# x loaded in 32-by-32 squares and turned on VectorE instead of TensorE, in a decoder block

## The reference

```python
h = rms_norm(x, norm_g) * (1.0 + scale) + shift        # scale, shift, gate from silu(c) @ w_ada + b_ada
proj = h @ w_in                                        # 1024 -> 3592 columns: u, z_pool, q, k, v, o, z_mlstm, gates
pool_out = causal_pool_mixer(u) * silu(z_pool)         # trailing means over 2/4/8/16 positions
qk = silu(causal_depthwise_conv(q, k))                 # width 4
hm = mlstm_chunkwise(q, k, v, gates)                   # 4 heads, chunks of 128 positions, one after the other
mlstm_out = head_norm(hm) * sigmoid(o) * silu(z_mlstm)
x = x + gate * (concat[pool_out, mlstm_out] @ w_out)
out = rms_norm(x, final_g)
```

## Time and profile before

| | |
|---|---|
| median of 3 runs | 1848.31 us (1847.39 to 1850.02) |
| profiled execution, its own time | 1848.88 us |
| span in the profile | 1847.1 us |
| TensorE busy | 1809.6 us (98%) |
| VectorE busy | 1013.3 us (55%) |
| ScalarE busy | 521.5 us (28%) |
| GpSimd busy | 262.1 us (14%) |
| granted TensorE clock, mean | 0.994 |
| bytes over the DMA queues | 336.85 MB, mean 182 GB/s |

### The profile page before, as it was taken

How to read it: one execution, slowest core, us unless ns; L and a number is a source line. 1 busy time by engine, 2 the same in 40 slices (tenths; PEclk the granted TensorE clock), 3 DMA queues, 4 the chain that set the end, 5 groups by cost and what they waited for, 6 DMA issues and landing times.

```text
span 1847.1 us, 25117 instructions
## 1 busy us (share of the span) xinstructions
PE 1809.6 (98%) x9537; PEld 1554.0 (84%) x9537; DVE 1013.3 (55%) x2247; ACT 521.5 (28%) x1054; POOL 262.1 (14%) x229
## 2 busy tenths in 40 slices
PE   6989999999999999999999999999999999999998
PEld 5878889888898888988888888888889888898886
DVE  6685684527736276353863357452673627735383
ACT  3344331332323132222222223132222313222221
POOL 3433222040210003000030001200022000300000
PEclk9899999999999999999999999999999999999999
DMA  9896735595256552665427653466535665266431
GB/s 329 272 313 181 239 116 181 165 327 194 93 189 194 191 186 85 211 203 178 155 91 242 203 193 104 163 204 216 179 99 189 187 198 189 78 212 202 150 124 69
DMA packets 144348, 336.85 MB, mean 182 GB/s; under 512 B 13068, under 2 KB 55012, under 8 KB 144228
## 3 DMA queue, kind: packets, MB, share of 16 engines
q1 hardware_dynamic: 129028, 312.56, 50.9%
q10 hardware_dynamic: 15200, 22.68, 4.1%
HBM read 288.86 MB, written 46.33 MB: 181 GB/s over the span
## 4 chain that ended last, share of the span: by engine, by line
PE 88%; DVE 7%; issue 2%; ACT 1%; DMA 1%; SPq 0%; POOL 0%; ACTq 0%; DVEq 0%; POOLq 0%
PE ps_acc L511 23%; PE ps_acc L513 23%; PE ps_acc L512 23%; PE ps_kv L511 2%; PE ps_kv L512 2%; PE ps_kv L513 2%; PE ps_num L728 1%; PE ps_kv L732 1%; PE ps_num L727 1%; PE ps_sco L708 1%; PE ps_num L524 1%; PE ps_num L511 1%; PE ps_num L513 1%; PE ps_num L512 1%; PE ps_bro L740 1%
## 5 line engine op out<-in xcount | busy, mean ns | idle before, releaser
L511 PE MATMUL ps_acc<-sb_hT_hi,sb_w_split 128*128 128x512 f32 x1536 | 608.9, 396 | 0.7 <-POOL sb_w_split L1104 0.7
L513 PE MATMUL ps_acc<-sb_hT_hi,sb_w_split 128*128 128x512 f32 x1536 | 599.6, 390 | 0.0
L512 PE MATMUL ps_acc<-sb_hT_lo,sb_w_split 128*128 128x512 f32 x1536 | 598.5, 390 | 0.0
L513 PEld LDWEIGHTS ps_acc<-sb_hT_hi,sb_w_split 128*128 128x128 f32 x1536 | 288.5, 188 | 62.1
L511 PEld LDWEIGHTS ps_acc<-sb_hT_hi,sb_w_split 128*128 128x128 f32 x1536 | 289.0, 188 | 58.5 <-POOL sb_w_split L1104 0.8
L512 PEld LDWEIGHTS ps_acc<-sb_hT_lo,sb_w_split 128*128 128x128 f32 x1536 | 289.1, 188 | 56.9
L1116 POOL TENSOR_TENSOR sb_h_rs<-sb_h_var,sb_mhalf 128x4 f32<-128x4 f32 x32 | 32.4, 1013 | 1019.1 <-DVE sb_h_var L1546 1019.1
L1104 POOL TENSOR_TENSOR sb_w_split<-sb_w_raw,sb_w_split 128x512 fp32r<-128x512 f32 (+1 forms) x64 | 89.0, 1400 | 183.4 <-ACT sb_w_split L812 183.3
L1454 DVE SCALAR_TENSOR_TENSOR sb_acc_cv<-sb_shifted,sb_par,sb_acc_cv 128x512 f32<-128x512 f32 x96 | 76.9, 801 | 60.8 <-ACT sb_acc_cv L964 58.3
L1480 DVE TENSOR_TENSOR sb_oz<-sb_tanh,sb_oz 128x512 f32<-128x512 f32 x32 | 22.2, 692 | 150.5 <-ACT sb_tanh L980 150.5
L511 PE MATMUL ps_acc<-sb_wo_hi,sb_mixm_hi 128*128 128x512 f32 x256 | 103.3, 404 | 0.0
(11 more groups left out here) (219 smaller groups left out, 2867.9 us busy)
## 6 DMA issues: line engine op xcount, KB each, us to landing
sb_w_split<-w_kept SPq DMA_DIRECT2D x328, 512.0 KB, 4.0
sb_w_split<-w_kept SPq DMA_DIRECT2D x56, 520.0 KB, 4.8
w_kept<-sb_w_split SPq DMA_DIRECT2D x40, 512.0 KB, 6.1
sb_x_res<-x SPq DMA_DIRECT2D x34, 512.0 KB, 5.5
sb_w_raw<-w_in SPq DMA_DIRECT2D x64, 256.0 KB, 5.1
out<-sb_qT SPq DMA_DIRECT2D x32, 512.0 KB, 2.9
sb_x_in<-x SPq DMA_DIRECT2D x30, 512.0 KB, 5.8
sb_ada_raw<-w_ada SPq DMA_DIRECT2D x8, 1024.0 KB, 9.6
```

What stands on the lines that cost most here:

```text
L511: pe.matmul(dst, st_hi, mv_hi, start=start, stop=False)
L512: pe.matmul(dst, st_hi, mv_lo, start=False, stop=False)
L513: return pe.matmul(dst, st_lo, mv_hi, start=False, stop=stop)
```

## The change

Block 0 keeps its way. For blocks 1 to 7, in the numbers of one chunk of 128 positions:

- `load_x` issues four DMAs in place of one, one for each quarter q of a feature group. Position 32 j + r goes to partition 32 q + r, with the 32 features of group k and quarter q laid at (k, j). On the memory side a contiguous run is 32 numbers, 128 bytes, so a chunk is 4096 runs instead of 128 rows.
- VectorE turns the chunk with one instruction that transposes 32-by-32 squares (`prep_turn`), into `kT` for even chunks and into the joined tile `dmat_q_in` for odd ones. TensorE's transposes are gone.
- A position's features now lie on four partitions. ScalarE squares in four instructions (`prep_sq`), and one matmul with the fixed matrix `same_row` (128 by 128, one where two partitions stand for the same row r) adds the four parts and spreads the sum (`x_sums`). Its output is 4 columns in a corner of `ps_kv`.
- `prep_var` reads that PSUM corner. The power on GpSimd is 4 columns wide. ScalarE scales, in four instructions, in place of VectorE's one.
- `prep_full` works in place in SBUF, not out of PSUM.
- `load_x` of chunk 2 now waits for `prep_turn(0)` on VectorE.

The matrix `same_row` is made once in the setup, out of the identity. `a_pad` shrinks to 32 columns.

```diff
+            def load_x(nb, c):
+                if c >= 2 or nb > 1:
+                    sp.wait_ge(x_turned, (nb - 1) * NC + c - 1)
+                else:
+                    sp.wait_ge(x_T, PREPS)
+                tokens = x[0, bass.ds(nb * BLK + c * P, P), :].rearrange("(j r) (k q n) -> r k j q n", r=32, q=4, n=32)
+                for q in range(4):
+                    dst = x_in[32 * q:32 * q + 32, c % 2, :].rearrange("r (k j n) -> r k j n", k=KT, j=NC)
+                    sp.dma_start(dst, tokens[:, :, :, q, :]).then_inc(x_loaded[c % 2], 16)
...
-            def prep(nb, p, src=x_in):
...
-                    last = pe.transpose(num[p % 2][:, chunk(i)], src[:, c % 2, chunk(k)], ident)
-                last.then_inc(x_T, 1)
+            def x_sums(nb, c):
+                if nb == 1 and c == 0:
+                    pe.wait_ge(same_row_ready, 1)
+                pe.wait_ge(x_sq_done, nb * NC + (c + 1))
+                pe.matmul(x_sums_at[c], same_row[:, :], x_sq[:, NC * (c % 2):NC * (c % 2) + NC], start=True,
+                          stop=True).then_inc(x_summed, 1)
...
                     numerator_and_update(j)
+                    if j >= 2 and not last_block:
+                        x_sums(b + 1, j - 2)
...
                 out_m(0)
                 out_m(1)
-                prep_next(0)
-                prep_next(1)
                 for i in range(8):
                     if i > 1:
                         out_m(i)
                     out_p(i)
                     if i == 1:
                         hm_transposed(3)
-                    if i in (2, 4, 6):
-                        prep_next(i)
-                        prep_next(i + 1)
+                    if i in (2, 4) and not last_block:
+                        x_sums(b + 1, i // 2 + 1)
...
+            def prep_sq(nb, c):
+                act.wait_ge(x_loaded[c % 2], x_count(nb, c))
+                for j in range(NC):
...
+            def prep_scale(nb, c):
+                act.wait_ge(x_rs_done, nb * NC + (c + 1))
+                for j in range(NC):
+                    at = NC * (c % 2) + j
+                    last = act.activation(x_blocks(c)[:, j, :, :], x_blocks(c)[:, j, :, :], ACT.Copy, scale=x_rs[:, at:at + 1])
+                last.then_inc(x_scaled, 1)
...
-                    prep_scale(b + 1, 1)
+                    prep_turn(b + 1, 0)
                 for i in range(8):
                     add_residual(i)
...
+                    if i in (3, 5) and not last_block:
+                        prep_var(b + 1, i // 2 + 1)
...
-                    if i in (1, 3) and not last_block:
-                        prep_scale(b + 1, 2 + i // 2)
+                    if i in (1, 3, 5) and not last_block:
+                        prep_turn(b + 1, i // 2 + 1)
```

More of the change, by code:

```diff
@@ L309, in chunk, with x_count, four_k, hT_part @@
             return slice(P * j, P * j + P)
+        def x_count(nb, c):
+            return 32 + 128 * (nb - 1) + 64 * (c // 2 + 1) if nb else 16 * (c // 2 + 1)
+        def four_k(c, half):
+            return x_turned_to[c % 2][:, 2 * half:2 * half + 2, :, :]
+        def hT_part(t, c, half):
+            return t[:, 4 * half:4 * half + 4, chunk(c)].rearrange("p (a b) t -> p a b t", b=2)
         def col(t, n, m=P):
@@ L685, in one_block @@
                         pe.wait_ge(a_ready, b + 1)
-                        pe.transpose(bro[:, chunk(0)], a_pad[:, :], ident).then_inc(bro_full, 1)
+                        pe.transpose(bro[0:32, chunk(0)], a_pad[:, :], ident).then_inc(bro_full, 1)
                     if t == 4:
@@ L1060, in one_block @@
                     act.activation(tanh[:, :], src[:, :], ACT.Tanh, scale=0.5).then_inc(tanh_ready, 1)
+                    if j == 3 and not last_block:
+                        prep_scale(b + 1, 0)
                     if first and m + 2 < UNITS:
@@ L1078, in one_block @@
                 squares(3)
+                if not last_block:
+                    prep_scale(b + 1, 1)
                 for i in range(8):
@@ L1152, in one_block @@
                         h_rsqrt(j - 1)
+                    if j == 3 and not last_block:
+                        x_rsqrt(b + 1, 0)
                     for n in range(m, m + 4):
@@ L1155, in one_block @@
                             low_w(n)
-                        if n == m + 2 and j >= 2 and not last_block:
-                            x_rsqrt(b + 1, j - 2)
                 h_rsqrt(3)
+                if not last_block:
+                    x_rsqrt(b + 1, 1)
                 for i in range(8):
@@ L1162, in one_block @@
                         prep_lo(b + 1, i + 1)
-                    if i in (1, 3) and not last_block:
-                        x_rsqrt(b + 1, 2 + i // 2)
+                    if i in (3, 5) and not last_block:
+                        x_rsqrt(b + 1, i // 2 + 1)
                     if i % 2:
@@ L1217, in prep_full @@
+            def prep_full(nb, p):
+                in_turn()
+                dve.wait_ge(x_turned, (nb - 1) * NC + (p // 2 + 1))
                 for i in range(4):
-                    k = 4 * (p % 2) + i
-                    last = V.tensor_scalar(full[p % 2][:, i, :], num[p % 2][:, chunk(i)], gain[:, k:k + 1], shift[:, k:k + 1],
-                                           ALU.mult, ALU.add)
+                    k, at = 4 * (p % 2) + i, four_k(p // 2, p % 2)[:, i // 2, i % 2, :]
+                    last = V.tensor_scalar(at, at, gain[:, k:k + 1], shift[:, k:k + 1], ALU.mult, ALU.add)
@@ L1536, in update_c @@
                     dve.wait_ge(kv_done, b * NC + (j + 1))
+                    if j >= 2 and not last_block:
+                        dve.wait_ge(x_summed, b * NC + (j - 1))
                     for h in range(NH):
@@ L1628, in one_block @@
                         head_norm(j - 1)
+                    if j == 3 and not last_block:
+                        prep_var(b + 1, 0)
                     in_turn()
@@ L1645, in one_block @@
                         m_low(0)
-                    if j >= 2 and not last_block:
-                        prep_var(b + 1, j - 2)
                     in_turn()
@@ L1656, in one_block @@
                         m_mixed(j - 1)
-                    if j == 2 and not last_block:
-                        prep_scale(b + 1, 0)
                 def add_residual(i):
@@ L1691, in one_block @@
                 head_var(3)
+                if not last_block:
+                    prep_var(b + 1, 1)
                 m_mixed(2)
@@ L1703, in one_block @@
                         out_norm(i // 2 - 1)
-                    if i in (1, 3) and not last_block:
-                        prep_var(b + 1, 2 + i // 2)
+                    if i in (3, 5) and not last_block:
+                        prep_var(b + 1, i // 2 + 1)
                     if i % 2:
```

111 lines of the change are left out of this document (57 added, 54 removed).

## The result

The changed kernel takes 1896.76 us (median of 4 runs, 1894.27 to 1898.65), the kernel before 1847.85 us (1846.78 to 1850.02) on the same chip. The ratio is 1.026, with a 95% interval of 1.0248 to 1.0272: slower by 49 us, where 58 were forecast. The profiled execution of the changed kernel took 1898.65 us, its span is 1896.9 us, and the mean granted TensorE clock is 0.98 (0.994 before). Of the runs further down, one execution of e2_rows_four took 2570 us at a mean granted clock of 0.66; no comparison rests on it.

What follows compares the result with a forecast made beforehand. TensorE's issue was taken to bound the kernel. Seven tails, each 8.2 us longer from the new wait and half clock less TensorE's net gain, add 58 us to 1848.9: 1907 profiled, 1906 us median, range 1856 to 1950.

Steps and rivals of the forecast that it cites:

- The likeliest case: Whole kernel: small-run loads make TensorE wait in seven tails, D between 2 and 7.5, 1875 to 1940 us; chance 0.69.
- What comes off TensorE and what is put on: TensorE, seven blocks: removing transposes gains 25 us, 28 small matmuls cost 6 us; 1830 us if nothing waited.
- The new wait: Behind output tile 4, TensorE's `x_sums` of chunk 3 waits 8.5 us for ScalarE's squares in every tail.
- D: Time the 16 DMA engines need for one chunk of x: 5.1 us, at 20 ns per 128-byte packet.
- The doubling: DMA loads of x: read-modify-write below 512 bytes, put with the rival of D = 15, 2045 to 2120 us; chance 0.08.
- Step 1: VectorE's turn of chunk 0 replaces `prep_scale` and takes 1.2 us; chunk 2's load is issued at 925.0, not 922.25.
- Step 4: From chunk 2's squares to the issue of chunk 3's load: 9.6 us instead of 10.1; gain and shift save 1.1.
- steps 2 and 4: Step 2, DMA loads in block 3's tail: fixed part 1.7 us, so chunk 2 lands at 926.7 + D.
- from S to R: Block 3's tail, from start of chunk 2's squares (931.8) until TensorE goes on behind its wait (952.6): 15.7 + D.
- The clock: TensorE behind each tail's wait of over 4 us runs at half clock, losing 2.6 us of work.
- What costs nothing: ScalarE's scaling, loads of chunks 0 and 1 ahead of weights (22 us of cover), their `x_sums`, `a_pad` and setup: no cost.
- Faster: Chunk 3's squares come before tile 4 ends at 944.1, so nothing waits: 1830 us; chance 0.06.

Runs made afterwards that it cites:

- e2_rows_four: The changed kernel with each chunk of x loaded by four DMAs of 32 whole rows, which alters the output: 1889.1 us.
- e11: The changed kernel with chunk 3's load before the first store, ScalarE's m_high and scaling before the squares, and chunk 3's small matmul behind tile 6: 1836.7 us.
- e1: The changed kernel with the small matmul of chunk 3 moved from behind output tile 4 to behind tile 6: 1891.7 us.
- e10: The changed kernel with ScalarE's m_high and scaling ahead of the squares, and chunk 3's small matmul behind output tile 6: 1835.8 us.
- e14: The changed kernel with chunk 3's load before the first store, plus needless VectorE rows behind the last norm to price gain and shift: 1845.9 us, one execution.
- e7: The changed kernel with 24 needless matmuls of 512 columns between output tile 4 and chunk 3's small matmul: 1885.2 us.
- e12: The changed kernel with chunk 3's load before the first store and each chunk loaded by one DMA of 128 rows, which alters the output: 1831.5 us.
- e8: The changed kernel with chunk 3's load, and the weight unit ahead of it, issued before the first store instead of behind it: 1837.2 us.
- e3: The changed kernel with each chunk of x loaded by one DMA of 128 whole rows, which alters the output: 1880.1 us.
- e9: The changed kernel with ScalarE's m_high of chunks 2 and 3 and scaling of chunk 2 ahead of the squares: 1890.6 us.
- e4: The kernel before, with only a wait added: TensorE waits behind output tile 4 for chunk 3's squares: 1868.0 us.

## Why the prediction was right, and where it was off

The forecast was 1906 us and the range 1856 to 1950. The likeliest case came about, by its own mechanism. That the total came so near is partly luck: the tails were forecast a third too long, and block 0 lost 5 us that were not forecast.

- **What comes off TensorE and what is put on.** 19 us over seven blocks were forecast, 2.7 a block. The steps of e11 and of before differ by 2.72. The parts are a little off and cancel: a small matmul moves the next by 0.14 us (925.45 to 925.59), not 0.22, so a group of transposes was worth 0.82 and not 0.9.
- **The new wait.** It is in the forecast place, with the forecast releaser, seven times, 6.1 us in block 3 and 6.3 in the mean (5.8 to 7.0), for 8.5. That this wait was the sole path was not right. The text had `m_high` and `m_low` on the way to the load, and did not ask what stands behind the late squares on ScalarE. e1 shows the second path and e10 that there are just these two. It changed no number of the forecast, but the cure that follows from the one-path reading gains only 5 us.
- **The price of a chunk, D.** This is one of the two terms of the sum that were mis-sized most. For a load with the DMA queues to itself (chunk 2's in block 3) the DMA view of the changed kernel shows:

```profile
DMA packets 4161, 0.53 MB, mean 76 GB/s; under 512 B 4160, under 2 KB 4160, under 8 KB 4160
...
q1 hardware_dynamic: 4160, 0.52, 48.2%
```

  48.2% of 16 engines over 7 us are 54 us for 4160 packets, 13 ns each and not 20, so D is 3.3 us and not 5.1 (over all the 128-byte packets of this trace the mean is 14.9 ns, which makes 3.8). The load of chunk 3 lands 7.5 us behind its issue, where 9 to 10 were forecast. The Trainium skill's page "DMA: Bandwidth & Descriptors", section "Why small descriptors are slow (HBM only)", led to an estimate of D = 2.5; measured it is between that and my value. Its section "Specifications" names a read-modify-write below 512 bytes. The doubling that the prediction made of it was not seen: a 128-byte packet takes less than the 22 ns of a 512-byte one.
- **Step 1, the turn.** 1.25 us, forecast 1.2.
- **Step 4, gain and shift.** Four were to take 0.8 us out of SBUF. They take 1.07 by themselves (e14), and once in eight VectorE stands 1.1 us behind GpSimd, so that eight take 3.25 us where 2.7 stood before and 1.6 were forecast: this is the other term. The Trainium skill states such a thing in "SBUF — State Buffer", section "Who interferes with whom": a VectorE instruction in a two-port mode, which `tensor_scalar` can enter, and a GpSimd one exclude each other for the whole instruction, and the one issued first goes first. The trace agrees with 1.32 us against 0.34; which mode the instruction was in, it does not show. The prediction had passed over it. The norm behind took 1.28 us (964.01), where it had taken 1.68 before (937.90, block 3), which gives 0.4 back. So the way from chunk 2's squares to chunk 3's issue is 10.7 us (955.66 to 966.34) and not 9.6. Chunk 2's squares, on the other side, did not wait for their load at all. The errors of steps 2 and 4 and of D partly cancel: from S to R went 19.9 us (955.66 to 975.59), forecast 20.8.
- **The clock.** 2.6 us a tail were forecast, and 2.4 measured: 19.1 us in the mean from the small matmul to the v matmuls, against 16.7 at full clock (e7). The 16.4 that the prediction took for these tiles was 0.3 short.
- **What costs nothing.** For the blocks behind block 0 this was right: e12 and e11 have the same step, and TensorE never waits for weights there, though the issues of eight DMAs take 9.5 us in block 1 too (416.10). For block 0 it was wrong: this cover was counted in block 3 and in time of the DMA engines. In block 0 the issues themselves hold SyncE for 12.8 us ahead of the weights. With the small runs gone, block 0 is 5.6 us shorter (e2).
- **The sum.** A tail costs 6.3 us of wait and 2.4 of clock, less the 2.7 gained: 6.0, where the steps show 6.1 and 8.2 were forecast. For six tails that is 13 us less. To it comes 13.4 us for block 0 in place of 8.2, of which 5 belong to the small runs ahead of the weights (5.6 by e2, less the 0.6 of any step). That leaves 49 for 58; without those 5 it would be 44.
- **The rivals.** Faster needed 3 us less on the way to chunk 3's load, and 1830 us was its time. The changed kernel did not do it. e8 does, with the load 6 us sooner against the store (5.3 ahead of it, not 1.0 behind), and runs in 1837. The rest to 1830 is block 0: 252.4 us, where the 249.3 of before less the gain of 2.7 would be 246.6.

Three kernels that compute the same layer beat both: e8, e10 and e11 are 0.6 to 0.8% faster than before. e8 needs the least.

## What to carry to other kernels

When a change lets an engine that works in order ask for data sooner, look at when those data are ordered, not only at how long they travel: here the load stood behind a store that had nothing to do with it, and moving it was worth 60 us. List everything that stands behind the late instruction on every engine before a cure is chosen, since two waits with one root each look harmless when only the other is removed. And count a cover in every stage, the first block with its own streams above all, in the time of the engine that issues as well as in that of the DMAs.

## What the runs showed of the hardware

- A 128-byte packet took 13 ns of a DMA engine when its load had the queues to itself and 14.9 in the mean of the whole trace, so a chunk of 4096 takes 3.3 to 3.8 us of all 16.
- The issue of a DMA of 1024 such runs held SyncE for 0.7 to 1.3 us in the tails (four in 2.8 to 5.0 us) and for 1.6 us with busy DMA engines in block 0 (eight in 12.8), where a DMA of 128 rows took 0.34 to 0.8.
- Four DMAs in place of one made the load land 1.5 us later with the same large rows (7.0 in e2 against 5.5 us in e3).
- VectorE's gain and shift out of SBUF waited out a GpSimd instruction of 1.31 us in all 28 chunks (1.32 us instead of 0.34); out of PSUM they did not.
- TensorE kept the full clock behind idle times of up to 2.3 us (e7: 16.7 us from the small matmul to the v matmuls in all seven tails). Behind every one of 3.7 to 7.0 us (changed kernel, e2, e3, e9) the same work took 18.3 to 19.8 us. In e4, with idle times of up to 2.7 us, the mean clock stayed at 0.993.
- The turn of 128 by 1024 float32 numbers in 32-by-32 squares takes 1.25 us on VectorE.
